# New counts of durations for a planner that orders the work of five engines

## What is computed

```python
# first layer, recurrence
sa = einsum('bhij,bhj->bhi', S, -kk_t)
S = S * w_t + sa * (kk_t * a_t) + v_t * k_t ; y = einsum('bhij,bhj->bhi', S, r_t)
# first layer, sparse attention, per block of 128 queries
score = einsum('bqh,bqhs->bqs', wi, relu(einsum('bqhd,bsd->bqhs', qi, k_idx)))
_, idx = top_k(where(causal, score, -inf), 256)
p = softmax(einsum('bqhr,bqkr->bhqk', qa, c_sel)) ; o = einsum('bhqk,bqkr->bqhr', p, c_sel)
x = x + concat([y_rwkv, y_attn]) @ w_out
# second layer
x = x + (concat([mla_attention(...), memory_cross_attention(...)]) * silu(gate)) @ w_out
```

## Time and profile before

| | us |
|---|---|
| median of 3 runs (lowest, highest) | 4830.44 (4821.56, 4830.96) |
| the profiled execution | 4825.16 |
| its span, first to last instruction | 4823.4 |

### The profile page before, as it was taken

How to read it: one execution, slowest core, us unless ns; L and a number is a source line. 1 busy time by engine, 2 the same in 40 slices (tenths; PEclk the granted TensorE clock), 3 DMA queues, 4 the chain that set the end, 5 groups by cost and what they waited for, 6 DMA issues and landing times. The chain is left out here.

```text
span 4823.4 us, 78905 instructions
## 1 busy us (share of the span) xinstructions
PE 4165.9 (86%) x32376; PEld 2814.8 (58%) x32376; DVE 2781.7 (58%) x5074; ACT 2156.7 (45%) x3170; POOL 1162.6 (24%) x919
## 2 busy tenths in 40 slices
PE   7998997768778877778678999798999999999879
PEld 6766765455555655556357788674444444444457
DVE  5556554557677767777564322345666666666443
ACT  4444443767777567776433322221233332333431
POOL 1111110253233434333111000001333333343200
PEclk9999998879889888888689999897999999999989
DMA  3333333112111111121066533663322323222143
GB/s 126 101 112 109 94 101 119 39 30 46 29 29 37 44 33 35 38 51 30 26 195 192 183 132 102 226 224 66 67 54 66 72 54 73 56 54 58 43 156 112
DMA packets 390601, 411.62 MB, mean 85 GB/s; under 512 B 116640, under 2 KB 288352, under 8 KB 389984
## 3 DMA queue, kind: packets, MB, share of 16 engines
q1 hardware_dynamic: 388144, 399.59, 28.8%
q10 hardware_dynamic: 2096, 6.99, 0.4%
HBM read 254.85 MB, written 151.62 MB: 84 GB/s over the span
## 5 line engine op out<-in xcount | busy, mean ns | idle before, releaser
L142 ACT ACTIVATE PT<-psum 128x1024 f32<-128x1024 f32 x384 | 372.2, 1021 | 896.4 <-PE psum L132 896.4
L170 DVE TENSOR_REDUCE m<-psum 128x1 f32<-128x1024 f32 x384 | 469.9, 1224 | 439.2 <-PE psum L132 439.0
L132 PE MATMUL psum<-xc,wah 128*128 128x512 f32 x1600 | 513.7, 402 | 1.5 <-DVE xc L146 1.5
L146 POOL TENSOR_TENSOR part<-PT 128x1024 f32<-128x1024 f32 x144 | 342.7, 2380 | 639.9 <-DVE all L146 445.6
L132 PE MATMUL psum<-PT,V 128*64 128x512 f32 x1536 | 370.5, 603 | 0.2 <-ACT PT L142 0.2
L143 ACT ACTIVATE bias<-score,cand,cols 128x2048 bf16<-128x2048 f32 (+6 forms) x217 | 314.3, 1448 | 114.5 <-DVE cand L158 111.1
L146 POOL TENSOR_TENSOR Lm<-gm,cst 64x512 f32<-64x512 f32 x192 | 257.8, 1343 | 412.5 <-PE psum L132 253.7
L143 ACT ACTIVATE sgn<-score,cand,cols 128x1920 bf16<-128x1920 f32 (+6 forms) x217 | 290.8, 1340 | 133.4 <-DVE cand L158 132.0
L132 PEld LDWEIGHTS psum<-xc,wah 128*128 128x128 f32 x1600 | 299.6, 190 | 77.3 <-issue 9.2
L132 PE MATMUL psum<-hc,w4h 128*128 128x512 f32 x1024 | 320.4, 394 | 11.6 <-ACT w4h L142 11.6
L132 PE MATMUL psum<-xc,wal 128*128 128x512 f32 x800 | 315.8, 395 | 0.0
(11 more groups left out here) (337 smaller groups left out, 9184.0 us busy)
## 6 DMA issues: line engine op xcount, KB each, us to landing
raw_a<-in_w_a SPq DMA_DIRECT2D x50, 512.0 KB, 4.0
raw_w<-in_w_in SPq DMA_DIRECT2D x32, 512.0 KB, 4.5
QNh<-scr_qnh SPq DMA_DIRECT2D x48, 256.0 KB, 5.0
QRh<-scr_qrh SPq DMA_DIRECT2D x96, 128.0 KB, 4.9
QNl<-scr_qnl SPq DMA_DIRECT2D x48, 256.0 KB, 7.1
QRl<-scr_qrl SPq DMA_DIRECT2D x96, 128.0 KB, 6.3
xin<-in_x SPq DMA_DIRECT2D x16, 512.0 KB, 3.5
scr_AR<-AR SPq DMA_DIRECT2D x32, 256.0 KB, 2.5
```

The costliest lines, as they stand in the source:

```text
L132: return self.e.matmul(out, a, b, start=start, stop=stop, skip_group_check=True)
L142: return self.e.activation(out, src, f, bias=bias, scale=scale)
L146: return self.e.tensor_tensor(out, a, b, op) if self.e else self.vector(out)
L170: return self.e.tensor_reduce(out, a, AX, op, negate=negate) if self.e else self.vector(a)
```

## The change

The counts of durations are replaced. On VectorE an operation has a larger fixed part and a smaller part per element, and the smallest is 0.22 us; on GpSimd and ScalarE likewise both parts move. On TensorE an fp32r product is counted by its columns alone, a float32 one gets a fixed part and is halved for 64 rows and again for 64 columns; a transpose is 0.17 instead of 0.12; each piece on TensorE costs 0.12 more. A signal is seen 0.2 us after its operation instead of 0.1, the end of a transfer 7.0 us after its issue instead of 4.0. No instruction, tile, buffer, lane or list of pieces is touched.

```diff
--- before.py
+++ after.py
@@ -117,27 +117,27 @@
         self.book.note("op", us, table)
         return Nothing()
 
-    def vector(self, ap, fixed=0.07, slope=0.0012):
+    def vector(self, ap, fixed=0.15, slope=0.00105):
         if self.name == "pool":
-            return self.idle(max(0.5, 0.1 + 0.0024 * each(ap)))
-        return self.idle(max(0.18, fixed + slope * each(ap)))
+            return self.idle(0.25 + 0.002 * each(ap))
+        return self.idle(max(0.22, fixed + slope * each(ap)))
 
     def dma(self, out, src):
         return self.e.dma_start(out, src) if self.e else self.idle(0.1, "dma")
 
     def mm(self, out, a, b, start=True, stop=True):
         if not self.e:
-            part = 2 if a.shape[0] <= 64 or each(a) <= 64 else 1
-            return self.idle(max(64, each(b)) * (0.00045 if a.dtype == FR else 0.0017) / part)
+            part = (2 if a.shape[0] <= 64 else 1) * (2 if each(a) <= 64 else 1)
+            return self.idle(0.00048 * each(b) if a.dtype == FR else 0.03 + 0.0019 * max(64, each(b)) / part)
         return self.e.matmul(out, a, b, start=start, stop=stop, skip_group_check=True)
 
     def turn(self, out, src, ident):
-        return self.e.transpose(out, src, ident) if self.e else self.idle(0.12)
+        return self.e.transpose(out, src, ident) if self.e else self.idle(0.17)
 
     def act(self, out, src, f, bias=0.0, scale=1.0, acc=None):
         if not self.e:
             table = {ACT.Sqrt: "root", ACT.Exp: "exp", ACT.Tanh: "exp"}.get(f)
-            return self.idle(0.15 + 0.0009 * each(out) + (0.2 if acc is not None else 0.0), table)
+            return self.idle(0.1 + 0.00098 * each(out) + (0.19 if acc is not None else 0.0), table)
         if acc is None:
             return self.e.activation(out, src, f, bias=bias, scale=scale)
         return self.e.activation(out, src, f, bias=bias, scale=scale, accum_out=acc)
@@ -164,13 +164,13 @@
         return self.e.memset(out, x) if self.e else self.vector(out)
 
     def recip(self, out, a):
-        return self.e.reciprocal(out, a) if self.e else self.vector(out, 0.1, 0.0065)
+        return self.e.reciprocal(out, a) if self.e else self.vector(out, 0.15, 0.0063)
 
     def reduce(self, out, a, op, negate=False):
         return self.e.tensor_reduce(out, a, AX, op, negate=negate) if self.e else self.vector(a)
 
     def scan(self, out, a, b, first, op0, op1):
-        return self.e.tensor_tensor_scan(out, a, b, first, op0, op1) if self.e else self.vector(out, 0.1, 0.0024)
+        return self.e.tensor_tensor_scan(out, a, b, first, op0, op1) if self.e else self.vector(out, 0.15, 0.0022)
 
     def addmax(self, out, a, b, acc):
         if not self.e:
@@ -230,13 +230,15 @@
             if not lanes[e][name]:
                 del lanes[e][name]
             last = t
+            if e == "pe":
+                t += 0.12
             for y in items:
                 if y[0] == "op":
                     if y[2] in ("exp", "root") and y[2] != table[e]:
                         table[e] = y[2]
                         t += 1.3
                     t += y[1]
-                    last = t + (4.0 if y[2] == "dma" else 0.1)
+                    last = t + (7.0 if y[2] == "dma" else 0.2)
                 elif y[0] == "up":
                     at[y[1]] = last
             free[e] = t
```

## The result

The changed kernel takes 4674.8 us (4671.6 to 4677.7) against 4830.7: the ratio is 0.9682, with a 95% interval from 0.9667 to 0.9697. The direction was right, and the size was not.

The account below looks back on a forecast made before the run. The prediction took the second stage's circular waits between in-order queues as the bound. Transfers -33 and TensorE's counts -32 gave -65 us, from 4825.2 to 4760, plus 5.3 for the median: 4766 us, range 4690 to 4870.

Parts of the forecast that it names:

- What bounds the kernel: Second stage, 1574 us: no engine full, in-order queues wait for each other, 373 us of TensorE's time go to waits.
- TensorE's counts: Second stage: planner saw TensorE at 0.66 of measured time, new 0.94; 32 us gain taken, ends 0 and 128.
- The clock: Second stage: the granted clock was to rise above 0.85, a sign without a term in the sum.
- Transfers: Second stage, loads into wu: 15 waits, 2.9 us less each; 22 to 44 us gain, 33 taken.
- the rival of a 7.0 that is too long: Pieces behind other, lone transfers are put back and eat the gain at wu; 32 us stay, 4798 us, chance 0.16.
- Semaphores and small operations, other engines: Search rounds counted 1.51 us against 1.27 measured, other engines' counts right before and after; taken at 0.
- The slower rival: Second stage: search rounds counted 0.24 us too long fall behind, masks come late; +80 us, 4910 us, chance 0.24.
- The first stage: TensorE counted 75 us higher there, side products perhaps placed late; taken at 0, with 15 us either way.
- The range: Whole kernel: 4690 to 4870 us, the high end taking in the slower half of the way to the slower rival.
- What would show it: Signs: second stage 1490 to 1530 us, clock above 0.85, wu waits under 25 us, mx waits not above 62.

Follow-up runs that it names:

- 1.27 of the true count: The changed kernel with all of TensorE's counts, the 0.12 us per piece too, 35% longer: 4801.8 us, ratio 0.9923.
- the run with TensorE undone: The changed kernel with TensorE's old counts put back: 4824.4 us, ratio 0.9987 to the kernel before.

## Why the prediction was wrong

*What bounds the kernel.* Right: the second stage, in which no engine is full and the queues wait for each other, holds 140 of the 147.7 us between the two profiles; the planned stages with a backlog on TensorE kept their time.

*TensorE's counts.* The mechanism was right, and the step that failed is its size, an eighth of the waits of rows 3: 32 us were taken, 140 (alone) or 147 (on top of the rest) were measured, and the upper end of 128 lies below both. (In the second stage of the profiles alone it is 119 and 129 us; the rest lies in other stages and in how single executions differ.) Three things went into that. The base was too small: the four groups of rows 3 are 255.6 us, but all rows that these two waits views list in the stage sum to 539.6, and the smaller groups (R, Xl, gm, rl and others) shrank as well. The share was too small: with TensorE's counts alone these waits fell by 263 us and the stage by 119, nearly a half and not an eighth; the prediction held the half for an extreme end, since a wait that goes is often replaced by another. And the yardstick is only good on one side: at 1.27 of the true count the same waits are low and the stage is long. Two other figures were at hand in the prediction: TensorE's count stood at 0.66, and TensorE was idle for 373 us. Of these, 103 came free; by what rule one could have told that share beforehand, no run shows.

*The clock.* It is missing in the sum. Of the stage's 140 us, 37 are TensorE's busy time, at a clock of 0.88 for 0.85. The prediction said that the clock would be above 0.85 and gave it no term. Here the idle time that went came with a higher clock and counted for about a third more than itself (37 on 103); as the table shows, this share does not hold for every run.

*Transfers.* The waits fell as forecast, by 43 us (44 was the full amount), and the time agrees: 33 us taken, 31 alone and 28 on top. Some of that agreement is luck. In the profiles the second stage, which was priced, got only 19 us (alone) and 22 us (on top) shorter, at or below the low end of 22; the rest came from stages taken at 0 and from how single executions differ. The landing is close to what was worked out; in the changed kernel one of the five waits that are left, start and length of the issues and of the first product:

```profile
1326.60 3.27 SPq L126 DMA_DIRECT2D bt<-scr_BT  x3
1329.91 2.60 SPq L126 DMA_DIRECT2D wu<-scr_VT  x4
...
1334.72 1.12 PE L132 MATMUL psum<-wu,gm 64*64 64x64 f32 x16 [5.02 <-DMA wu<-scr_VT]
```

From 1326.60 to 1334.72 are 8.1 us, which 7.7 doesn't quite cover; where the rest of these 5.0 us comes from is not shown (TensorE's count, a little short still, would work that way). What TensorE waits for is the last of seven in line, and the runs side with the row on it. The Trainium skill's page "DMA: Bandwidth & Descriptors" (section "Anatomy of one DMA — SWDGE (gpsimd) path") gives one transfer on GpSimd's path about 2.0 us fixed and its bytes over 436 GB/s, an estimate of 2.2 us for 64 KB. The 2.9 us of the earlier trace rows are 0.7 above that, for one transfer; it decides nothing for the seven in line. Counts far beyond, 10.0, cost nothing, so that the rival of a 7.0 that is too long fell too.

*Semaphores and small operations, other engines.* Taken at 0. On top of TensorE's and the transfers' counts that is right within what was measured: 0.9701 with signals at 0.1 and 0.9677 with the old counts of the three engines, against 0.9682. Without one of these two parts they cost 22 and 13 us together (above), which the prediction did not see. The slower rival, by which rounds counted 19% too long let the masks come late, did not come: the waits for mx fell from 62.0 to 33.7 us, and in the run with TensorE undone they were 51.5.

*The first stage.* Taken at 0 with 15 us either way; it ends 1 us earlier. Its parts are less calm: the second stage's first product starts at 836.7 us before, at 829.7 with TensorE's counts alone, at 841.1 with the transfers' alone, at 846.6 in the changed kernel without TensorE's counts. In the changed kernel, losses and gains of up to 10 us cancel; with TensorE's counts at 1.35 the stage loses 32 us.

*The range.* Its low end, 4690, was put above the forecast's own bound of 4638 with the reason that both gains at their full ends together were unlikely. That reason was beside the point: the transfers came in the middle of their range, and TensorE's counts, beyond the end of theirs, reach 4692.9 us alone. Of the signs under "What would show it" one failed, the second stage's length: 1434 us, where 1490 to 1530 had been forecast.

## What to carry to other kernels

Where a planner orders in-order queues, compare for each engine the sum of its counted time in a stage with its busy time there: TensorE counted a third too fast cost 3% of this kernel, TensorE counted 9% too slow nothing that could be measured, and changing the length of single operations by up to 3% at random, in one draw, nothing either. Waits in a circle show the fault, but a small share of the largest groups of waits is no price for it: sum all groups, and set the engine's idle time beside the sum. Look at the other side, too: TensorE at 1.27 of its time lost 2.4 of the 3.2% that the change had gained. Allow for TensorE's clock where idle time goes, in the range at least. And take parts out as well as putting them in alone: only the pair showed that two parts priced at 0 cost something while another part was missing.

## What was not expected

That the order is so insensitive near true counts: between 0.94 and 1.09 of TensorE's time, between 7.0 and 10.0 us for a transfer, with or without the new counts of three engines, all ratios lie between 0.9675 and 0.9682. And that TensorE's busy time for the same 15,850 records in the second stage lay between 1157 and 1208 us, at granted clocks from 0.84 to 0.91. Mostly it is shorter where the clock is higher, but in the run at 1.27 it is 1208 us at 0.89, longer than 1200 at 0.85; why, these runs don't show.
